# Exchanges through DRAM begun by GpSimd instead of SyncE in a two-layer decoder trunk

## What is computed

```
h = h + W_out(concat(gated branches(rms_norm(h) @ w_in)))
even layer: gated DeltaNet (8 heads of 128), a causal depthwise convolution of 31 taps with LayerNorm,
            softmax attention (4 heads of 256) to 256 memory tokens
odd layer:  stick-breaking attention (16 heads of 128):
            z = q k^T / sqrt(128);  weights[t,s] = sigmoid(z_ts) * prod_{s<j<t} (1 - sigmoid(z_tj));  o = weights v
            and the same memory attention
```

## Time and profile before

| | us |
|---|---|
| median of three runs | 1323.17 (1322.90 to 1323.55) |
| the profiled execution | 1322.03 |
| its span | 1320.3 |
| PE busy in the span | 1313.2 |
| DVE, ACT, POOL busy | 989.5, 741.2, 105.2 |

### The profile page before, as it was taken

The page is one execution under the profiler, slowest core; times in us unless marked ns, Lnnn a source line. Parts: engine busy times, 40 slices in busy tenths (PEclk is TensorE's granted clock), DMA queues, the critical chain, the costliest instruction groups (busy, mean ns, idle before and its releaser), DMA issues.

```text
span 1320.3 us, 18059 instructions
## 1 busy us (share of the span) xinstructions
PE 1313.2 (99%) x6653; PEld 1117.0 (85%) x6653; DVE 989.5 (75%) x1526; ACT 741.2 (56%) x1159; POOL 105.2 (8%) x103
## 2 busy tenths in 40 slices
PE   9999999999999999999999999999999999999998
PEld 8998899888888888888888888888888888888887
DVE  5557589898898998686666477798788788667563
ACT  6546633476445556576336456847757658554341
POOL 2000301003020100000000020020110200000000
PEclk9999999999999999999999999999999999999999
DMA  9655464555756996666755755765775766977652
GB/s 315 200 174 182 145 196 136 151 177 160 229 172 192 309 283 191 219 196 198 215 176 148 250 172 163 224 206 162 228 211 153 238 196 188 283 212 224 202 191 80
DMA packets 160432, 262.38 MB, mean 199 GB/s; under 512 B 25008, under 2 KB 43353, under 8 KB 160345
## 3 DMA queue, kind: packets, MB, share of 16 engines
q1 hardware_dynamic: 157625, 256.51, 62.6%
q10 hardware_dynamic: 2720, 4.72, 1.1%
HBM read 245.85 MB, written 15.34 MB: 198 GB/s over the span
## 4 chain that ended last, share of the span: by engine, by line
PE 79%; DVE 1%; POOL 0%; issue 0%; DVEq 0%
PE job L1873 49%; PE job L1883 24%; PE mixer L2098 1%; PE mixer L2086 1%; PE mixer L1894 1%; PE mixer L2108 1%; PE mixer L2116 1%; PE mixer L2003 0%; PE mixer L2107 0%; PE mixer L2118 0%; PE mixer L1983 0%; DVE cvr L1632 0%; DVE wlo L1384 0%; PE mixer L2016 0%; PE mixer L1991 0%
## 5 line engine op out<-in xcount | busy, mean ns | idle before, releaser
L1873 PE MATMUL job<-whi,xhi 128*128 128x512 f32 x1532 | 610.7, 399 | 0.0
L1873 PE MATMUL job<-whi,xlo 128*128 128x512 f32 x1532 | 597.3, 390 | 0.0
L1384 DVE TENSOR_TENSOR wlo<-raw,whi 128x1024 fp32r<-128x1024 f32 x431 | 529.1, 1247 | 75.4 <-ACT whi L1042 74.4
L1042 ACT ACTIVATE whi<-raw 128x1024 fp32r<-128x1024 f32 x431 | 444.9, 1055 | 209.5 <-PE job L1883 158.6
L1883 PE MATMUL job<-wlo,xhi 128*128 128x512 f32 x1532 | 409.9, 389 | 0.0
L1883 PEld LDWEIGHTS job<-wlo,xhi 128*128 128x128 f32 x1532 | 287.6, 188 | 60.5
L1873 PEld LDWEIGHTS job<-whi,xhi 128*128 128x128 f32 x1532 | 287.9, 188 | 57.6
L1873 PEld LDWEIGHTS job<-whi,xlo 128*128 128x128 f32 x1532 | 288.0, 188 | 57.4
L1632 DVE SCALAR_TENSOR_TENSOR cvr<-cvr,vt 128x255 f32<-128x255 f32 (+14 forms) x240 | 106.3, 500 | 0.2
L1870 PE MATMUL job<-xhi,whi 128*128 128x256 f32 x376 | 94.1, 288 | 0.4 <-DVE xlo L1429 0.4
L1870 PE MATMUL job<-xlo,whi 128*128 128x256 f32 x376 | 92.1, 283 | 0.0
(11 more groups left out here) (297 smaller groups left out, 964.4 us busy)
## 6 DMA issues: line engine op xcount, KB each, us to landing
raw<-in_od_w_in_dram SPq DMA_DIRECT2D x160, 512.0 KB, 3.8
raw<-in_ev_w_in_dram SPq DMA_DIRECT2D x143, 512.0 KB, 4.1
raw<-in_ev_w_out_dram SPq DMA_DIRECT2D x48, 512.0 KB, 5.3
raw<-in_od_w_out_dram SPq DMA_DIRECT2D x48, 512.0 KB, 5.1
raw<-in_w_mem_kv_dram SPq DMA_DIRECT2D x32, 512.0 KB, 4.7
proj<-turned_blocks SPq DMA_DIRECT2D x48, 128.0 KB, 4.6
turned_blocks<-proj SPq DMA_DIRECT2D x8, 512.0 KB, 4.5
turned_weights<-mix SPq DMA_DIRECT2D x16, 192.0 KB, 4.8
```

The lines of the kernel that those rows point to most:

```text
L1042: act(whi[:, c % RING, :, :], raw[:, c % RAWS, :, :], ACT.Copy).then_inc(s_hi, 1)
L1384: vec.tensor_tensor(wlo[:, c % RING, :, :], raw[:, c % RAWS, :, :], whi[:, c % RING, :, :].bitcast(F32), ALU.subtract).then_inc(s_lo, 1)
L1873: mm(pj[j % 2][n][:, :], x[:, s, cols], h, start=first, stop=False)
```

## The change

The six functions that begin an exchange's transfers (`do_xw`, `do_xr`, `do_sw`, `do_sr`, `do_aw`, `do_ar`) move from SyncE's program to GpSimd's. Their waits, addresses and semaphores are the same, only the engine that waits and issues is another. GpSimd walks the list and has few steps in it, so it comes to a load step as soon as its store step is done and then waits for the landing, where SyncE came to it after the weight loads in between. The list itself is not changed. SyncE keeps the weight chunks, the inputs and the small transfers of the inversion (`inZ` to `inD`).

```
-            def do_sw(h):
-                sp.wait_ge(s_sbcp, h + 1)
-                if h >= 2:
-                    sp.wait_ge(*weights_exchanged(h - 2))
-                sp.dma_start(bass.AP(dram_w, 49152 * (h % 2), [[384, 128], [1, 384]]), weights_out).then_inc(s_sx[h % 2], 16)
...
-            steps = {"aw": do_aw, "ar": do_ar, "sw": do_sw, "sr": do_sr, "load": load_chunk, "inZ": do_inZ, "inA": do_inA, "inB": do_inB, "inC": do_inC, "inD": do_inD,
-                     "xw": do_xw, "xr": do_xr}
+            steps = {"load": load_chunk, "inZ": do_inZ, "inA": do_inA, "inB": do_inB, "inC": do_inC, "inD": do_inD}
...
+            def do_sw(h):
+                gp.wait_ge(s_sbcp, h + 1)
+                if h >= 2:
+                    gp.wait_ge(*weights_exchanged(h - 2))
+                gp.dma_start(bass.AP(dram_w, 49152 * (h % 2), [[384, 128], [1, 384]]), weights_out).then_inc(s_sx[h % 2], 16)
+
+            def do_sr(h):
+                gp.wait_ge(*weights_exchanged(h, 1))
+                if h >= 2:
+                    gp.wait_ge(s_sbop, h - 1)
+                for b in range(4):
+                    gp.dma_start(weights_in[h % 2][32 * b:32 * b + 32].rearrange("p a m j -> p a (m j)"),
+                                 bass.AP(dram_w, 49152 * (h % 2) + 96 * b, [[384, 32], [12288, 4], [1, 96]])).then_inc(s_sx[h % 2], 16)
...
-            steps = {"rstd": do_rstd, "dnG": do_dnG, "inW": do_inW, "d4x": do_d4x, "lnc": do_lnc, "d6": do_d6, "sbk": do_sbk, "sbn": do_sbn,
+            steps = {"xw": do_xw, "xr": do_xr, "sw": do_sw, "sr": do_sr, "aw": do_aw, "ar": do_ar, "rstd": do_rstd, "dnG": do_dnG, "inW": do_inW, "d4x": do_d4x, "lnc": do_lnc, "d6": do_d6, "sbk": do_sbk, "sbn": do_sbn,
```

More of the change, by code:

```diff
@@ L840, in do_inD @@
                 sp.dma_start(tinv8, rows_t).then_inc(s_inD, 16)
[L842 to L854, removed]
@@ L1014, in do_sbn, with do_xw @@
                                             ALU.mult).then_inc(s_sbn, 1)
-            steps = {"rstd": do_rstd, "dnG": do_dnG, "inW": do_inW, "d4x": do_d4x, "lnc": do_lnc, "d6": do_d6, "sbk": do_sbk, "sbn": do_sbn,
+            def do_xw(e):
+                gp.wait_ge(*blocks_turned(e))
+                if turn_no[e] >= 3:
+                    gp.wait_ge(s_xg[turn_no[e] % 3], 80 * (turn_no[e] // 3))
+                gp.dma_start(bass.AP(dram_x, 131072 * e, [[1024, 128], [1, 1024]]), stage[e]).then_inc(s_xg[turn_no[e] % 3], 16)
@@ new lines, in do_xr @@
+            def do_xr(e):
+                gp.wait_ge(*exchanged(e, 1))
+                if TURNED[e] in MQJOB[:4]:
+                    gp.wait_ge(s_mqs, order[MQJOB.index(TURNED[e])])
+                for b in range(4):
+                    gp.dma_start(landed(e)[32 * b:32 * b + 32, :].rearrange("p (a n) -> p a n", a=4),
+                                 bass.AP(dram_x, 131072 * e + 256 * b, [[1024, 32], [32768, 4], [1, 256]])).then_inc(s_xg[turn_no[e] % 3], 16)
+            def do_sw(h):
[3 more added lines that the diff above has]
+                gp.dma_start(bass.AP(dram_w, 49152 * (h % 2), [[384, 128], [1, 384]]), weights_out).then_inc(s_sx[h % 2], 16)
@@ new lines, in do_sr, with do_aw @@
+            def do_sr(h):
+                gp.wait_ge(*weights_exchanged(h, 1))
+                if h >= 2:
+                    gp.wait_ge(s_sbop, h - 1)
+                for b in range(4):
+                    gp.dma_start(weights_in[h % 2][32 * b:32 * b + 32].rearrange("p a m j -> p a (m j)"),
+                                 bass.AP(dram_w, 49152 * (h % 2) + 96 * b, [[384, 32], [12288, 4], [1, 96]])).then_inc(s_sx[h % 2], 16)
+            def do_aw(n):
+                gp.wait_ge(s_ptp, n + 1)
+                if n >= 2:
+                    gp.wait_ge(*probs_exchanged(n - 2))
+                gp.dma_start(bass.AP(dram_p, 65536 * (n % 2), [[512, 128], [1, 512]]), probs_out).then_inc(s_px[n % 2], 16)
@@ new lines, in do_ar @@
+            def do_ar(n):
+                gp.wait_ge(*probs_exchanged(n, 1))
+                if n % 4 >= 2:
+                    gp.wait_ge(s_maop, 2 * n - 2)
+                elif n < 4:
+                    gp.wait_ge(s_mqT, 8)
+                else:
+                    gp.wait_ge(s_xl, F_ODD + 8)
+                o, v = 512 * (n % 2), (pflat[:, 2048:3072], mflat[:, 0:1024])[n // 4]
+                for b in range(4):
+                    gp.dma_start(v[32 * b:32 * b + 32, o:o + 512].rearrange("p (a n) -> p a n", a=4),
+                                 bass.AP(dram_p, 65536 * (n % 2) + 128 * b, [[512, 32], [16384, 4], [1, 128]])).then_inc(s_px[n % 2], 16)
```

## The result

The kernel after takes 1327.56 us in the median of 7 runs (1325.44 to 1327.73), the kernel before 1323.11 in 7 runs beside it (1322.78 to 1323.55). The ratio is 1.0028, with a 95% interval of 1.0017 to 1.0039: slower, by 4.4 us between the medians and by 2.2 to 5.2 us by the interval. The profiled execution took 1327.73 us, its span is 1326.0 us.

The account below looks back on a forecast made before the run. TensorE was taken to bound the kernel. From 1322.03 us, adding 0 for SyncE's freed queue, 0.3 for weight, 0 for probability and 0.1 for block exchanges gave 1322.4 us, 1323.6 on the runs' scale; range 1321.4 to 1350.

Parts of the forecast that it names:

- no change that can be told: Whole kernel: the time stays within 1322 to 1325 us, a possible gain of at most 1.8 us included; chance 0.55.
- Slower: Whole kernel: the change makes it slower, by GpSimd as bottleneck (0.34) or VectorE holding GpSimd up (0.07); chance 0.41.
- A: Weight exchanges: GpSimd becomes their bottleneck, the fourth head of each group comes late; 1344 us at 1.3 us per issue; chance 0.34.
- B: DMA issues on GpSimd: VectorE holds GpSimd up while it sets a DMA up, 0.7 us per issue; 1392 us; chance 0.07.
- TensorE is the bound, SyncE's freed queue gains nothing: Whole kernel: TensorE is busy 1313.2 of 1320.3 us; work taken off SyncE gains 0, at most 1.8 us.
- c = 1.0 us: GpSimd: the price of beginning one store or load of an exchange, taken as 1.0 us.
- rival A's formula: Weight exchanges: the fourth head of a group is late by 20 issue costs less 19.7 us, with SyncE's landings.
- Weight exchanges: 16 stick-breaking heads in groups of four: fourth head's loads 0.3 us late; 0.3 us for all groups, between 0 and 1.2.
- Block exchange across the second inversion: Delta rule's second inversion: store and loads go ahead of GpSimd's masks; costs 0, at worst 1.6 us, taken as 0.1.
- by 365: Second inversion: GpSimd's third mask ending by 365 us was one sign that the forecast is right.
- The other blocks have an idle GpSimd around them and uses that lie further off; I count 0: All block exchanges but the one at the second inversion: moving them to GpSimd costs 0 us.

## Why the prediction was right, and where it was wrong

The measured time, 1327.6 us, lies in the range, in the part above the forecast's own (1322 to 1325), and the case I held likeliest, no change that can be told, is not what came. Slower had 0.41. It came neither by A nor by B of the rivals, but by a step that I had priced at nothing. That the range holds it is luck: the part of it above 1325 was there for A.

**TensorE is the bound, SyncE's freed queue gains nothing: right.** SyncE's waits for exchanges are gone, and what they made room for is waited away at the raw slots:

```profile
SPq L793 <- DVE wlo L1383: 1082.1, 418, 11.6
```

935.2 us before. TensorE's other waits are unchanged within 0.2 us. Worse, the freed queue was the loss: a SyncE that no longer stands still begins weight loads ahead of the exchange and beside it.

**c = 1.0 us: wrong in size, on the harmless side.** It is 0.55 us, nearer to SyncE's 0.43 than to GpSimd's powers, and it hardly spreads:

```profile
L993 POOL DMA_DIRECT2D cvr<-turned_weights x32: 548/548/566, 832.9 to 1132.0; - x32
```

The store of weights takes 0.56 and the longest of all 180, a block store, 0.79 us. With c = 0.55 rival A's formula gives 20 x 0.55 - 19.7 = -8.7 us: never late. This also settles B. VectorE was busy for 75% of the span, and beside it the 64 loads of weights differ by 0.02 us and all 180 issues by 0.24, where the masks differ by 0.9. The rule of the Trainium skill (SBUF — State Buffer, SBUF: two separate sides), by which an operation with two inputs doesn't keep GpSimd from writing descriptors, agrees with that.

**Weight exchanges: right in sign, wrong in the small number.** I had the fourth head 0.3 us late. Its loads were begun from 860.15 to 862.32 and TensorE took it at 869.72 (L2115), with no wait; by the median landing of 3.9 us that is about 4 us early. GpSimd never held the heads of that group up, it waited 1.4 to 2.4 us for VectorE before each store behind the first. The landings themselves were taken well: 4.1 us for a store (I took 4.8), 3.9 for a load (3.6).

**Block exchange across the second inversion: right.** The third mask ended at 365.2, where "by 365" had been the sign, in an execution that stood 0.9 us behind that of before. The loads were begun ahead of it without holding it, for it still waited 0.4 us for VectorE:

```profile
361.19 2.24 POOL L979 DMA_DIRECT2D proj<-turned_blocks  x4 [4.10 <-DMA turned_blocks<-proj]
363.79 1.41 POOL L930 TENSOR_TENSOR reg<-hid,mix 128x512 f32<-128x512 f32 x1 [0.36 <-DVE mix L1533]
```

**"The other blocks have an idle GpSimd around them and uses that lie further off; I count 0": this step failed.** An idle GpSimd says nothing of a landing, and how far off the uses were I had read for none of them. Exchange 4 had 14 us and used 12.9. The second thing that failed with it is the median as the price of a landing. Even had I looked here, SyncE's medians would have given 5.0 + 0.7 + 4 x 1.0 + 3.2 = 12.9 us, or 13.9 with the 4.6 us that block loads took in the median in place of the weights' 3.6: under the 14, so no loss. A landing is no property of the transfer. It depends on what has been begun ahead of it: line L979 has 2.9/5.5/9.1 us from issue to landing (min/median/max) in after. I had written that it "may be less, since the exchanges no longer stand in one queue with the 512 KB weight loads". That held for the stores of weights (4.1 us against 4.8), but it has the sign wrong for the loads of blocks, 5.5 us against 4.6 in the median. In SyncE's queue the four loads stood ahead of the next weight loads, and behind a pause of 3.9 us that SyncE's own wait had made; in another queue, nothing keeps weight loads from being begun first. The Trainium skill (DMA: Bandwidth & Descriptors, Queues, rings and completion order) says that each DMA engine takes turns between the queues that have work for it, a packet at a time. The mixed packets of after from 472 to 479 us agree with that. That the loads' first packet starts only 1.7 to 2.8 us after the first load, though nothing of their own queue stands ahead, against 1.3 in the runs in which SyncE waits until they have been begun or have landed, is more than that rule says; and weight loads begun 0.15 us behind were harmless, since their packets started when most of the exchange's had. The measurement decides: behind is harmless, ahead is not.

**The clock was in no term.** A wait of 3.0 us cost 4.7 by the windows and 4.9 by the matmuls' begins.

What stays open: why weight packets already begun in one queue hold up the first packet of another. The windows of after from 464 to 476 us move 284 to 401 GB/s, by which one weight load of 512 KB is 1.3 to 1.8 us of all the engines (an estimate), so one or two of them are of the size of the delay; but no run changed the size of what was ahead. Open is also why it hit only this exchange: that the others were in time I read from TensorE's waits and from the run with exchange 4 alone on SyncE, not by how much.

## What to carry to other kernels

When a transfer moves to a queue of its own, look up what its old queue did for it: what it stood ahead of, and what the old engine did not begin while it waited. For every moved exchange read the slack from its own rows (here 1.1 us in one of 36), and price the landing by what will have been begun ahead of it, not by a median. If the transfer must win against bulk loads, it was enough here that the bulk engine was held until the transfer had been begun; it need not wait for the landing. Here that only gave back the time of before.

## What the runs showed that I had not expected

- A DMA of 128 short runs costs GpSimd 0.55 us to begin, against 0.43 us for SyncE, with almost no spread (0.548 to 0.566 over 32).
- Four loads of 128 KB reached their use in 4.8 to 5.2 us on SyncE's and on GpSimd's queue alike when no weight load had been begun in the 4 us ahead, and in 8.4 to 9.8 us on GpSimd's and ScalarE's alike with one begun less than 3 us ahead.
- After TensorE had been idle for 3.0 us, its granted clock was 0.52 and 0.63 over the next two windows of 2 us: the clock adds more than half of the stall again. With 41.7 us of waits in 15 heads TensorE was busy for 23.2 us more.
- A power of 16 columns took GpSimd 2.9 us or 3.8 us, for the same instruction with the same inputs.
